# Router reordered, phases folded on the scalar engine, and ten idle products on constants

## The reference

```
first_block:  h = rms_norm(x);  u, z, q, k, v, ... = split(h @ w_in)
              y_s = state space branch of u: x[t] = lam * x[t-1] + B u[t], y = Re(C x) + d u, for 64-wide states
              y_a = dilated attention of q, k, v (q and k normalized and partly rotated)
              x = x + (sigmoid(r_s) * (y_s ...) + sigmoid(r_a) * (y_a ...)) @ w_o
second_block: a gated recurrence and a differential attention, then x = x + mixed @ w_out
hier_moe:     xt = rms_norm(x);  g = argmax(xt @ w_rg + b_rg)            # 4 groups of 8 experts
              two largest of (xt @ w_re + b_re) inside g, softmax weights times the group's softmax weight
              out[token] += weight * ((silu(xt @ w1[e]) * (xt @ w3[e])) @ w2[e])   # 32 experts
```

## Time and profile before

| | |
|---|---|
| median of three runs | 1237.9 us (1235.53 to 1239.94) |
| the profiled execution | 1241.23 us, of which the span is 1239.2 us |
| TensorE busy | 993.8 us (80%) |
| VectorE busy | 469.4 us (38%) |
| ScalarE busy | 204.8 us (17%) |
| GpSimd busy | 170.5 us (14%) |
| bytes read from HBM | 292.90 MB |
| the longest shares of the chain that ended last | transfers of expert units 29%, TensorE 7%, VectorE 1% |

### The profile page before, as it was taken

How to read it: one execution, slowest core, us unless ns; L and a number is a source line. 1 busy time by engine, 2 the same in 40 slices (tenths; PEclk the granted TensorE clock), 3 DMA queues, 4 the chain that set the end, 5 groups by cost and what they waited for, 6 DMA issues and landing times. The chain is left out here.

```text
span 1239.2 us, 11138 instructions
## 1 busy us (share of the span) xinstructions
PE 993.8 (80%) x4394; PEld 484.9 (39%) x4394; DVE 469.4 (38%) x787; ACT 204.8 (17%) x384; POOL 170.5 (14%) x126
## 2 busy tenths in 40 slices
PE   5998887989798999899989995776766665666655
PEld 4644433444687744654544443421212121212211
DVE  6959999990752120327253313110101010110101
ACT  2222333321341101131221112000000000000000
POOL 2645555552100000100000001000000000000000
PEclk9999988989898999899999997897979797988897
...
GB/s 367 154 136 76 129 68 79 125 68 174 76 77 128 136 143 128 136 141 135 136 68 136 128 429 138 195 430 426 428 429 428 429 428 429 428 427 430 428 428 232
DMA packets 22456, 294.50 MB, mean 238 GB/s; under 512 B 2992, under 2 KB 3184, under 8 KB 4880
## 3 DMA queue, kind: packets, MB, share of 16 engines
...
HBM read 292.90 MB, written 1.05 MB: 237 GB/s over the span
## 5 line engine op out<-in xcount | busy, mean ns | idle before, releaser
L1868 PE MATMUL psum<-mem 128*32 128x512 f32 x1024 | 139.9, 687 | 74.3 <-DMA mem<-in_experts 69.3
L286 PE MATMUL psum<-mem,hT 128*128 128x512 f32 x416 | 186.8, 607 | 1.3 <-ACT xres L604 1.3
L293 PE MATMUL psum<-mem,hT 128*128 128x512 f32 x288 | 135.4, 629 | 4.3 <-ACT mem L604 3.4
L286 PE MATMUL psum<-mem 128*128 128x512 f32 x288 | 125.2, 593 | 2.4 <-ACT mem L1302 1.5
L1881 PE MATMUL psum<-mem 128*32 128x512 f32 x512 | 86.5, 810 | 48.6 <-DMA mem<-in_experts 44.8
L286 PEld LDWEIGHTS psum<-mem,hT 128*128 128x128 f32 x416 | 79.5, 194 | 98.2 <-issue 98.1
L1868 PEld LDWEIGHTS psum<-mem 128*32 128x32 f32 x1024 | 32.9, 118 | 173.0 <-DMA mem<-in_experts 108.6
L293 PEld LDWEIGHTS psum<-mem,hT 128*128 128x128 f32 x288 | 58.8, 208 | 76.1 <-issue 76.0
L286 PEld LDWEIGHTS psum<-mem 128*128 128x128 f32 x288 | 54.2, 190 | 69.0 <-issue 65.1
L300 PE MATMUL psum<-hT,mem 128*128 128x256 f32 x320 | 75.2, 395 | 4.3 <-PEq L1140 4.3
L300 PEld LDWEIGHTS psum<-hT,mem 128*128 128x128 f32 x320 | 62.7, 198 | 14.4 <-DVE hT L1137 4.6
...
## 6 DMA issues: line engine op xcount, KB each, us to landing
...
xres<-in_x SPq DMA_DIRECT2D x2, 1024.0 KB, 8.3
hT<-in_xT SPq DMA_DIRECT2D x1, 1024.0 KB, 9.0
...
out<-xres SPq DMA_DIRECT2D x1, 1024.0 KB, 5.5
...
```

The source lines that it names most:

```text
L286: ins = pe.matmul(dst, lhs[:, k, P * i:P * i + P], w[:, k, c0:c0 + 512], start=(k == 0), stop=(k == nk - 1))
L293: ins = pe.matmul(dst, tokens[:, k, i], w[:, k, :], start=(k == 0), stop=(k == KD - 1))
L1868: ins = pe.matmul(banks[m // 4][32 * q:32 * q + 32, :], xgT[:, k, 32 * q:32 * q + 32], w[:, q, FF * kk:FF * kk + FF], start=(k == 0), stop ...
```

## The change

- **Phases.** `whole_turns` and `take_turns_off` go. The plain sum of angles is handed to ScalarE, which folds it with absolute values and constant offsets (`folds`) and then takes two sines: six operations instead of three.
- **Logits.** The four turned quarters of x and the logits alternate, and ScalarE's third copy stands before its last square.
- **Router.** `aexp`, the choice without weights, is made first, for both halves of the tokens in one operation; the exponentials and weights come after the first selection. GpSimd's two operations and its load go: x is scaled only, and the gain is applied when VectorE copies the gathered tile. Counts go to another bank.
- **Idle products.** TensorE does ten 128x256 products on constants before it waits for `chosen`.
- **Gather and experts.** Products of the first units wait for half of `xg_` only, the weights are turned after unit 3, the next group's selection is made in advance.
- **End.** The units of w2 are laid out by column half (the host packs them so), so that the first half of the columns is combined before the last unit; four stores of 256 KB replace one of 1 MB.

```
+put("folds", np.array([-0.25, -0.5, -HALF_PI])[None, :])
...
-    act.activation(sin_t[:, b], phase[:, b], ACT.Sin, scale=TURN)
-    link(act, act.activation(abs_t, phase[:, b], ACT.Abs), act1)
-    link(act, act.activation(cos_t[:, b], abs_t, ACT.Sin, scale=-TURN, bias=halfpi), trig_ready)
+    mark(act.activation(sin_t[:, b], phase[:, b], ACT.Abs, bias=quarter_off), act1)
+    link(act, act.activation(cos_t[:, b], phase[:, b], ACT.Abs), act1)
+    mark(act.activation(sin_t[:, b], sin_t[:, b], ACT.Abs, bias=half_off), act1)
+    link(act, act.activation(cos_t[:, b], cos_t[:, b], ACT.Abs, bias=half_off), act1)
+    act.activation(sin_t[:, b], sin_t[:, b], ACT.Sin, scale=TURN, bias=halfpi_off)
+    link(act, act.activation(cos_t[:, b], cos_t[:, b], ACT.Sin, scale=TURN, bias=halfpi_off), trig_ready)
...
-        done = mark(dve.tensor_tensor(ph[:, w], bc(fa[:, 2 * pr + w, :].unsqueeze(2), [P, 16, 16]),
-                                      bc(fb[:, 2 * pr + w, :].unsqueeze(1), [P, 16, 16]), ALU.add), dve1)
...
-def whole_turns(pr):
-    return mark(dve.tensor_scalar(rot_im, phase[:, pr % 2], ROUND, ROUND, ALU.add, ALU.subtract), dve1)
-def take_turns_off(pr):
-    mark(dve.tensor_tensor(phase[:, pr % 2], phase[:, pr % 2], rot_im, ALU.subtract), phase_ready)
+        ins = dve.tensor_tensor(ph[:, w], bc(fa[:, 2 * pr + w, :].unsqueeze(2), [P, 16, 16]),
+                                bc(fb[:, 2 * pr + w, :].unsqueeze(1), [P, 16, 16]), ALU.add)
+    mark(ins, phase_ready)
...
-    more = pr + 1 < PAIRS
-    if more:
-        summed = angle_sums(pr + 1)
+    if pr + 1 < PAIRS:
+        angle_sums(pr + 1)
...
-    if more:
-        after(summed)
-        turns = whole_turns(pr + 1)
...
-    if more:
-        after(turns)
-        take_turns_off(pr + 1)
...
-    if more:
-        dve.wait_ge(phase_ready.sem, pr + 2)
...
-after(angle_sums(0))
-after(whole_turns(0))
-take_turns_off(0)
-dve.wait_ge(phase_ready.sem, 1)
+angle_sums(0)
...
-turned_x(act, TP_R + 2)
+    if n == 2:
+        turned_x(act, TP_R + 2)
...
-turn_x(0, 1)
-turn_x(1, 1)
+def logits(c, i):
+    tp.after_read(pe, TP_R + 2 * c + i)
+    for k in range(4 * c, 4 * c + 4):
+        ins = pe.matmul(banks[4 + i][:, 0:36], hT[:, k, P * i:P * i + P], wr[:, k, :],
+                        start=(k == 0), stop=(k == KD - 1))
...
-for i in range(2):
-    tp.after_read(pe, TP_R + 2 + i)
-    for k in range(KD):
-        ins = pe.matmul(banks[4][:, 36 * i:36 * i + 36], hT[:, k, P * i:P * i + P], wr[:, k, :],
-                        start=(k == 0), stop=(k == KD - 1))
-ins.then_inc(logits_full, 1)
+turn_x(0, 1)
+logits(0, 0)
+logits(0, 1)
+turn_x(1, 1)
+logits(1, 0)
+logits(1, 1).then_inc(logits_full, 1)
...
+def store(n):
+    i, c = n % 2, n // 2
+    sp.dma_start(out[0, P * i:P * i + P, 512 * c:512 * c + 512], xres[:, i, 512 * c:512 * c + 512]).then_inc(out_done, 16)
+for n in range(4):
+    sp.wait_ge(added, 4 * (N_GROUPS - 1) + n + 1)
+    store(n)
...
-sp.dma_start(out[0].rearrange("(i p) n -> p i n", p=P), xres[:, :, :]).then_inc(out_done, 16)
-sp.wait_ge(out_done, 16)
...
-load(gainr_, A["norm_moe_2"][0].partition_broadcast(P))
...
-for i in range(2):
...
-    pool.tensor_tensor(xperm[:, i].rearrange("p k q -> p q k"), scaled[:, i, :].rearrange("p (q k) -> p q k", k=KD), gq,
-                       ALU.mult).then_inc(xn3_ready, 1)
...
+    for n in range(4):
+        store(n)
+    sp.wait_ge(out_done, 128)
...
-act.wait_ge(exp_in3, 1)
-act.activation(gexp, gexp, ACT.Exp).then_inc(exp_out3, 1)
+    act.activation(xn[:, i, :], xres[:, i, :], ACT.Copy, scale=rstd3[:, i:i + 1]).then_inc(xn3_ready, 1)
+act.activation(warm, eps, ACT.Exp)
...
+act.activation(gexp, gexp, ACT.Exp)
...
-    act.wait_ge(gather_full, it * 2 + 2)
-    act.activation(xg_[:, 512:1024], banks[5], ACT.Copy).then_inc(xg_high, 1)
...
+for n in range(10):
+    pe.matmul(banks[6][:, 0:256], ident, con[:, 0:256], start=True, stop=True)
...
-pe.matmul(banks[5][:, 32:64], ones, aexp[:, 0, :], start=True, stop=False)
-pe.matmul(banks[5][:, 32:64], up, aexp[:, 1, :], start=False, stop=True)
-pe.matmul(banks[5][:, 64:96], ones, aexp[:, 0, :], start=True, stop=False)
-pe.matmul(banks[5][:, 64:96], ones, aexp[:, 1, :], start=False, stop=True).then_inc(places_full, 1)
+pe.matmul(banks[5][:, 32:64], up, aexp[:, 1, :], start=True, stop=False)
+pe.matmul(banks[5][:, 32:64], ones, aexp[:, 0, :], start=False, stop=True).then_inc(places_full, 1)
+pe.matmul(banks[7][:, 0:32], ones, aexp[:, 0, :], start=True, stop=False)
+pe.matmul(banks[7][:, 0:32], ones, aexp[:, 1, :], start=False, stop=True).then_inc(counts_full, 1)
...
-    pe.wait_ge(selw_ready, it + 1)
-    for i in range(2):
-        ins = pe.transpose(banks[6][:, P * i:P * i + P], selw_[:, P * i:P * i + P], ident)
-    ins.then_inc(selT_full, 1)
...
-    pe.wait_ge(xg_high, it + 1)
...
+        if m == 2:
+            pe.wait_ge(xg_high, it + 1)
...
+        if m == 3:
+            pe.wait_ge(selw_ready, it + 1)
+            for i in range(2):
+                ins = pe.transpose(banks[6][:, P * i:P * i + P], selw_[:, P * i:P * i + P], ident)
+            ins.then_inc(selT_full, 1)
...
-        k = m - 8
-        for c in range(2):
+        c = (m - 8) // 2
+        for kk in range(2):
+            k = 2 * (m % 2) + kk
...
-                                w[:, q, 512 * c:512 * c + 512], start=(k == 0), stop=(k == 3), tile_position=(0, 32 * q))
+                                w[:, q, 512 * kk:512 * kk + 512], start=(k == 0), stop=(k == 3), tile_position=(0, 32 * q))
...
-    pe.wait_ge(selT_ready, it + 1)
-    for n in range(4):
-        if n == 0:
-            pe.wait_ge(y_low, it + 1)
-        if n == 2:
-            pe.wait_ge(y_high, it + 1)
-            pe.wait_ge(added, it * 4 + 1)
-        if n == 3:
-            pe.wait_ge(added, it * 4 + 2)
-        pe.matmul(banks[6 + n % 2], selT_[:, P * (n % 2):P * (n % 2) + P], y_[:, 512 * (n // 2):512 * (n // 2) + 512],
-                  start=True, stop=True).then_inc(combined, 1)
+        if m >= 10:
+            if m == 10:
+                pe.wait_ge(selT_ready, it + 1)
+                pe.wait_ge(y_low, it + 1)
+            else:
+                pe.wait_ge(y_high, it + 1)
+            for n in (2 * c - 2, 2 * c - 1) if m == 10 else (2, 3):
+                if n >= 2:
+                    pe.wait_ge(added, it * 4 + n - 1)
+                pe.matmul(banks[6 + n % 2], selT_[:, P * (n % 2):P * (n % 2) + P], y_[:, 512 * (n // 2):512 * (n // 2) + 512],
+                          start=True, stop=True).then_inc(combined, 1)
...
+by_group = lambda ap: ap.rearrange("p i (g e) -> p i g e", g=4)
+of_group = bc(goh.unsqueeze(3), [P, 2, 4, 8])
...
-dve.wait_ge(exp_out3, 1)
-step(dve.tensor_reduce(gsum, gexp, AX.X, ALU.add))
-step(dve.reciprocal(gw, gsum))
-for i in range(2):
-    step(dve.tensor_tensor(prodg[:, i], lge[:, i], bc(goh[:, i].unsqueeze(2), [P, 4, 8]), ALU.mult))
-    step(dve.tensor_reduce(eg[:, i], prodg[:, i].rearrange("p g e -> p e g"), AX.X, ALU.add))
+step(dve.tensor_tensor(prodg, lge, of_group, ALU.mult))
+step(dve.tensor_reduce(eg, prodg.rearrange("p i g e -> p i e g"), AX.X, ALU.add))
...
+step(dve.tensor_tensor(s8, oh1, oh2, ALU.add))
+dve.tensor_tensor(by_group(aexp), bc(s8.unsqueeze(2), [P, 2, 4, 8]), of_group, ALU.mult).then_inc(chosen, 1)
...
-dve.wait_ge(exp_out3, 2)
+dve.wait_ge(chosen, 1)
+dve.wait_ge(places_full, 1)
+step(dve.tensor_tensor(place[:, :, 0:EXPERTS], aexp, banks[5][:, 0:64].rearrange("p (i n) -> p i n", i=2), ALU.mult))
+slots = bc(C("iota")[:, 1:SLOTS + 1].unsqueeze(1).unsqueeze(1), [P, 2, 4, SLOTS])
+def select(four):
+    return dve.tensor_tensor(sel, slots, bc(place[:, :, four].unsqueeze(3), [P, 2, 4, SLOTS]), ALU.is_equal)
+select(slice(0, GROUP_OF)).then_inc(sel_ready, 1)
+dve.wait_ge(exp_out3, 1)
+step(dve.tensor_reduce(gsum, gexp, AX.X, ALU.add))
+step(dve.reciprocal(gw, gsum))
...
-step(dve.tensor_tensor(s8, oh1, oh2, ALU.add))
...
-for dst, src in ((wexp, w8), (aexp, s8)):
-    for i in range(2):
-        step(dve.tensor_tensor(dst[:, i].rearrange("p (g e) -> p g e", g=4), bc(src[:, i].unsqueeze(1), [P, 4, 8]),
-                               bc(goh[:, i].unsqueeze(2), [P, 4, 8]), ALU.mult))
...
-dve.wait_ge(places_full, 1)
...
-step(dve.tensor_tensor(place, aexp, pl, ALU.mult))
...
+step(dve.tensor_tensor(by_group(wexp), bc(w8.unsqueeze(2), [P, 2, 4, 8]), of_group, ALU.mult))
+dve.wait_ge(counts_full, 1)
...
+    dve.wait_ge(sel_ready, it + 1)
...
-    for i in range(2):
-        ins = dve.tensor_tensor(sel[:, i], bc(slots.unsqueeze(1), [P, 4, SLOTS]),
-                                bc(place[:, i, four].unsqueeze(2), [P, 4, SLOTS]), ALU.is_equal)
-    ins.then_inc(sel_ready, 1)
-    dve.wait_ge(sel_ready, it + 1)
-    for i in range(2):
-        ins = dve.tensor_tensor(selw[:, i], sel[:, i], bc(wexp[:, i, four].unsqueeze(2), [P, 4, SLOTS]), ALU.mult)
-    ins.then_inc(selw_ready, 1)
-    dve.wait_ge(gather_full, it * 2 + 1)
```

(9 more changed lines are left out.)

71 lines of the change are left out of this document (32 added, 39 removed).

## The result

The changed kernel takes 1203.6 us (median of 4 runs, 1202.3 to 1205.4), the kernel before 1238.9 in the same job (1235.5 to 1245.5): a ratio of 0.971, 95% interval 0.968 to 0.974, or 35.3 us less. Forecast were 28.8 us and 1209. The profiled execution took 1204.45 us, 36.8 less than the one of before.

A forecast was written before the change was run, and what follows sets the result against it. It took VectorE to bound the scan stage, a serial chain the router, and DMA the expert stream before a serial tail. Scan 8.2, router 15.3 and end 5.3 sum to 28.8 us off 1237.9: 1209.1 us, range 1200 to 1217.

The forecast's parts named there:

- What bounds the kernel: DMA bounds from the first used unit on, so time saved ahead moves the whole stream; VectorE bounds the scan stage.
- Turns 3 to 14: Scan stage, two VectorE steps removed: 0.71 us saved in six uncontended turns, some 0.6 in six contended; 8.2 us in all.
- first rival: Scan stage: VectorE gains the removed steps' full durations, 19.6 us, giving 1197.7 us; chance 0.12.
- TensorE feeds the first three pairs late: Start of the scan stage: VectorE's savings in the first turns were counted at nothing.
- A sign that did come: Scan turns: VectorE waiting for ScalarE at L963 would prove a term wrong.
- I cost this at nothing: Scan stage, six ScalarE operations: copies up to 1.9 us late after odd turns, absorbed by TensorE's 18.0 us of waits.
- the slower case: Scan turns: the sines become the bound; slower than before from 9.7 us for the six operations, 1247.5 at 10.5; chance 0.02.
- if that cover goes: Scan stage: if TensorE's waits don't absorb late ScalarE copies, six waits cost up to 11 us and cancel the term.
- Router: Logits to first unit: 1.1 + 9.8 + 2.5 + 2.9 - 1.0 = 15.3 us saved; bounds 6.1 to 17.8.
- second rival: Router: the ten idle products run at half clock rate, 3.8 us more lost, 1212.9 us; chance 0.15.
- fifth rival: Router: the ten products don't hold the clock, gather stays at 6.24 us, 2.1 lost, 1211.2; within the forecast's 0.60.
- The end: Behind the last unit: last store issued 3.5 us earlier and landing 1.8 us faster, 5.3 us saved (3.5 to 6.6).

## Why the prediction was right, point by point, and which terms were mis-sized

**What bounds the kernel.** Right: the stream moved as a whole with the first unit, and VectorE set the turns.

**Turns 3 to 14.** Forecast 8.2 us and 29.5 us for two pairs; 8.9 and 29.44. VectorE's lead grew from 3.93 us at turn 3 to 12.86 at turn 15, by 0.68 in an uncontended turn (0.71 forecast) and by about 0.75 in a contended one (0.6 to 0.65). The scans' growth to 3.49 us shows why not the full pitches of 19.6 us (first rival): the whole stage gave 13.5 and 13.7 us in the kernels with the phases undone and alone, and 2.5 and 4.1 of them had been gained before the inputs of pair 2. L966 and L970, whose two inputs both lie in SBUF, take 1.80 and 1.68 us beside GpSimd; L963, with one of them in PSUM, takes 0.68. On this point the rows agree with the Trainium skill (GPSIMD Engine Reference, section 1, Specifications), which has VectorE's steps with two SBUF inputs contend with GpSimd.

**The step that failed: "TensorE feeds the first three pairs late, so only turns 3 to 14 count".** It holds for pairs 2 and 3, not for pair 1, whose inputs waited 2.37 us for VectorE, and the clock behind the wait cost 1.7 more. 3.9 us between these two profiles. The kernel with the first three pairs left as they were confirms the way it goes (4.8 us in the medians, 3.25 at the end of the stage), not the size, which differs from kernel to kernel with how much of VectorE's work falls beside GpSimd: L935 took 2.27 us in the changed kernel and 4.30 in the one without the idle products, with the same scan code. The fault was to read TensorE's waits from 93 us on only.

**A sign that did come.** The prediction said that a VectorE waiting for ScalarE at L963 would prove a term wrong. It waits 4.02 us at the first turn. What was wrong is the premise that the phase is ready a turn ahead: pair 0 has no turn before it. The term itself, ScalarE at nothing, is off by some 1.0 us at most, as named below.

**The clock, left out of the sum.** The last fills went from 16.76 to 14.01 us, and a wait of 2.89 us that had stood before their inputs is gone; the attention block gained 2.4 us. The fills at the end of the stage took 16.62 us in the kernel with the phases undone and 14.01 in that with the phases alone, so the gain on the fills follows from the phases; of the attention block's 2.4 no run shows the cause apart (a run of 128 products took 30.82 us before and 29.58 after).

**ScalarE.** "I cost this at nothing" was right within what the runs can tell: without the added operations the stage ends 1.0 us earlier and the median is the same. But the cover was thin. The prediction put the slower case's point at six operations of 9.7 us, since it looked for VectorE waiting for the sines. Four more operations (2.6 us) cost 13 us long before that, by the copies behind them, which the text had named and priced at up to 11 us "if that cover goes". TensorE's 18 us of waits weren't spare: most lay at other places than the new waits for copies, which came with the second fill behind an odd turn (127.52 and 156.96 us), where TensorE had not waited before.

**Router.** Forecast 15.3, measured 16.8. The steps to the choice took 5.06 us (4.8 forecast), places and selection 1.74 (2.0), gather to first unit 4.1 (4.3). Of the difference 1.0 is the idle products: 1.0 lost in the forecast, nothing in the trace, since none of them ran at the half clock (1.00 from 742.8 to 747.5 us); the second rival did not occur. The fifth rival (they don't hold the clock) did not occur in this profile either, where they are worth 2.0 us; in one other kernel it did, see the end.

**The end.** Forecast 5.3, measured 2.8: 2.9 behind the last unit, 0.1 lost in the stream. The last store was to be issued 5.5 us after the last unit's landing: it is 5.4 where TensorE was in time (1186.73 to 1192.17 in the kernel with one fill moved), 7.2 in the profiled execution of the changed kernel, through the first half's products at the lower clock. The store itself was to save 1.8 us; four stores against one gave 1.6 to 1.9 in the profiles, though not by the landing time alone. The section that the prediction set beside it (the Trainium skill, DMA: Bandwidth & Descriptors, Anatomy of one DMA) is on transfers that GpSimd issues. These stores are issued by SyncE, so their landing times say nothing against its figure.

So the gain was 8.0 us above the forecast in the profiles and 6.5 in the medians: in the profiles 3.9 more from the first turns, 0.7 from the others, 4.4 from the clock, 1.5 from the router, and 2.5 less from the end.
